# Context expert rows summed on TensorE inside two-head attention steps: a hybrid HGRN2, attention and PEER layer pair on one core

## What is computed

```python
def attend(q, k, v):                       # latent: k, v = 512 latent + 128 cached context positions
    def block(qi):
        s = jnp.einsum('bqkgd,bskd->bkgqs', qi, k).astype(jnp.float32) * ATTN_SCALE
        p = jax.nn.softmax(s, axis=-1).astype(v.dtype)
        return jnp.einsum('bkgqs,bskd->bqkgd', p, v)
...
def peer_mixer(h, w_query, sub_keys, u_tab, v_tab):
    q = (x @ w_query).reshape(T, PEER_HEADS, 2, PEER_HALF)
    ...                                    # two top-16 lists, their 256 sums, top 16: expert, gate
    def block(args):
        xb, eb, gb = args
        a = jax.nn.gelu(jnp.einsum('td,thkd->thk', xb, u_tab[eb]), approximate=False)
        return jnp.einsum('thk,thkd->td', gb * a, v_tab[eb])
```

## Time and profile before

| | |
|---|---|
| median of 3 runs | 5605.55 us (5605.12 to 5608.3) |
| span of the profiled execution | 5604.2 us, the median of the runs is 1.35 us above it |
| TensorE busy, 17704 instructions | 4557.5 us, 81% |
| VectorE busy | 3712.8 us, 66% |
| ScalarE busy | 1424.7 us, 25% |
| GpSimd busy | 2184.8 us, 39% |
| moved by DMA | 1703.74 MB, mean 304 GB/s |

### The profile page before, as it was taken

One profiled execution on the slowest core, in us unless ns is written; L12 is line 12 of the kernel. 1 busy time (PEld: TensorE's weight loads), 2 busy tenths in 40 slices (PEclk: granted clock), 3 DMA queues, 4 the chain that ended last, 5 costly groups with the idle time before them and its releaser, 6 DMA issues. The chain is left out here.

```text
span 5604.2 us, 60591 instructions
## 1 busy us (share of the span) xinstructions
PE 4557.5 (81%) x17704; PEld 2520.6 (45%) x17704; DVE 3712.8 (66%) x7028; ACT 1424.7 (25%) x3646; POOL 2184.8 (39%) x1826
## 2 busy tenths in 40 slices
PE   7889988888676777777787999888795878777776
PEld 6556655646343322222265566556463433223222
DVE  2357768867788766754532677788677877677545
ACT  2112213411011333333321112134100113333333
POOL 0002124642656454455400121246336554444554
PEclk9999998999888999999999999989897989999999
DMA  7755336785989999999967543457869889999998
GB/s 267 266 184 194 122 131 219 255 331 215 384 318 346 421 419 418 418 421 416 383 225 275 197 163 117 175 191 254 330 243 365 326 311 421 421 419 411 421 421 345
DMA packets 296082, 1703.74 MB, mean 304 GB/s; under 512 B 33360, under 2 KB 43216, under 8 KB 175696
## 3 DMA queue, kind: packets, MB, share of 16 engines
q0 software_dynamic: 258048, 1342.29, 61.3%
q1 hardware_dynamic: 23712, 338.18, 15.8%
q10 hardware_dynamic: 14000, 19.42, 1.0%
HBM read 1694.52 MB, written 5.24 MB: 303 GB/s over the span
## 5 line engine op out<-in xcount | busy, mean ns | idle before, releaser
L368 POOL DMA_INDIRECT arena<-in_peer_uv,eidx x1024 | 1184.3, 1157 | 1458.7 <-POOLq L367 1195.4
L2151 DVE SCALAR_TENSOR_TENSOR arena<-arena 128x1024 f32<-128x1024 f32 x384 | 470.6, 1225 | 349.9 <-DMA arena<-in_peer_uv,eidx 338.4
L861 PE MATMUL banks<-arena 128*128 128x512 f32 x896 | 502.1, 643 | 237.7 <-PEq L1473 234.2
L411 POOL DMA_INDIRECT arena<-in_peer_uv,eidx x384 | 490.3, 1277 | 501.0 <-POOLq L410 475.7
L863 PE MATMUL banks<-arena 128*128 128x512 f32 x896 | 477.8, 616 | 0.0
L834 PE MATMUL banks<-ring,arena 128*128 128x512 f32 x864 | 383.7, 599 | 110.0 <-PEq L816 110.0
L463 ACT ACTIVATE arena<-arena 128x1 f32<-128x1 f32 (+1 forms) x772 | 156.9, 203 | 1035.4 <-ACTq L462 1033.6
L861 PEld LDWEIGHTS banks<-arena 128*128 128x128 f32 x896 | 155.3, 198 | 549.7 <-issue 549.2
L468 ACT ACTIVATE arena<-ident,arena 128x128 f32<-128x128 f32 x832 | 333.6, 401 | 234.7 <-ACTq L467 230.2
L2151 DVE SCALAR_TENSOR_TENSOR ring<-ring,arena 128x1024 f32<-128x1024 f32 x192 | 235.4, 1226 | 211.1 <-DMA ring<-in_peer_uv,eidx 209.9
L2161 DVE SCALAR_TENSOR_TENSOR arena<-arena 128x1024 f32<-128x1024 f32 x256 | 306.9, 1225 | 95.3 <-DMA arena<-in_peer_uv,eidx 80.8
(11 more groups left out here) (303 smaller groups left out, 7763.1 us busy)
## 6 DMA issues: line engine op xcount, KB each, us to landing
ring<-in_wblk SPq DMA_DIRECT2D x160, 2048.0 KB
arena<-in_peer_uv,eidx POOLq DMA_INDIRECT x1408
arena<-in_lnrows ACTq DMA_DIRECT2D x6, 1024.0 KB, 9.5
arena<-in_sk ACTq DMA_DIRECT2D x4, 1024.0 KB, 7.4
hT<-in_peer_uv,eidx POOLq DMA_INDIRECT x192
ring<-in_peer_uv,eidx POOLq DMA_INDIRECT x192
x<-in_x_sample ACTq DMA_DIRECT2D x1, 2048.0 KB, 28.6
out<-arena ACTq DMA_DIRECT2D x4, 512.0 KB, 7.5
```

The lines of the kernel that those rows point to most:

```text
L368: nc.gpsimd.indirect_dma_start(grow[j], None, ins["peer_uv"], bass.IndirectOffsetOnAxis(ap=eidx[:, n, r:r + 1].bitcast(U32), axis=0)).then ...
L411: nc.gpsimd.indirect_dma_start(gslot[j], None, ins["peer_uv"].rearrange("(e h) d -> e (h d)", h=2), bass.IndirectOffsetOnAxis(ap=eidx[:, n ...
L861: nc.tensor.matmul(banks[:, b, :], diag[n], row[:, 0:CB], start=start, stop=stop, skip_group_check=True).then_inc(diag_used, 1)
L2151: V.scalar_tensor_tensor(u, u, 1.0, h2[:, t - 2, :], ALU.mult, ALU.mult, accum_out=av[:, r:r + 1])
```

## The change

- **Steps for units.** An attention step treats both heads of a pair for 128 queries: 32 steps instead of 64 units. Scores of the two heads are issued in turn (rows 0 to 63 and 64 to 127 of the array); the weighing has the values as the stationary side (64 columns), so the result comes out transposed, head by head in 64 partitions of bank 5. The reciprocal sums are spread by two more matmuls, copied by ScalarE (`sums_out`) and multiplied in by VectorE (`finish`) straight into `oattT`. The output transposes and GpSimd's staging of queries go; queries are transposed from `qkv`, one block in each step. The probabilities' ten transposes go through bank 4 alone in three parts (4, 4, 2 and the query block).
- **Sums of context rows on TensorE.** Ids are permuted (`ctx_ids`, `dot_column`) so that one gather brings four slots for 32 tokens. Four such gathers make a group. `ctx_group(n)` multiplies each with a 128 x 32 weight block (`spread_weights`) into its own 32 partitions of banks 6 and 7: eight matmuls of 512 columns in each step. VectorE's v-row additions and `merge_sums` go.
- **Dots** use `rep`, a replica of 32 rows of `h2c` in all four partition quarters, fetched by four DMAs from ScalarE's queue for every 16 dots. They use six slots, at the end three. Sum rows use seven slots, four of them in `ring[:, 1]`. SyncE therefore holds the next block for slot 1 until the last group is done (`ring_given`).
- **Halves.** Dots, GELU and weights are handled in two halves of 64 slots; the first half's GELU comes at the start of stage 5.
- **Row counts.** 16 rows in stage 3 instead of 24, 7 in each head instead of 6, then 22 and 4; the last 30 dots in steps 0 to 12. No row is left for `one_mix(one_tile)`.
- **Scalings.** The four constant scalings of a head's gates (`decays`) move from VectorE to ScalarE (`keys_in`).

```diff
-GATE_ROWS = 24
-HEAD_ROWS = 6
+GATE_ROWS = 16
+HEAD_ROWS = 7
 KEY_ROWS = 22
 QUERY_ROWS = 4
-UNIT_ROWS = 2
+STEP_ROWS = [3] + [2] * 6 + [3] * 2 + [2] * 3 + [3]
+DOT_SLOTS, LATE_SLOTS, SUM_SLOTS = 6, 3, [3, 4, 5, 12, 13, 14, 15]
...
                 for n, b in enumerate(CTX_BLOCKS + LAT_BLOCKS + ONE_BLOCKS + GRP_BLOCKS):
+                    if n == len(CTX_BLOCKS + LAT_BLOCKS) + 1:
+                        assert n % 2 == 1
+                        sp.wait_ge(ring_given, 1)
+                        sp.sem_inc(ring_given, -1)
                     load(n % 2, l * NB + b)
...
+            def ctx_rows_in():
+                dot_rows(0, dots_end + LATE_SLOTS)
+                pool.wait_ge(ring_idle, 1)
+                pool.sem_inc(ring_idle, -1)
+                sum_rows(0, len(SUM_SLOTS))
+                dots, sums = dots_end + LATE_SLOTS, len(SUM_SLOTS)
+                for n in range(1, STEPS):
+                    last = min(SLOTS, dots_by(n) + LATE_SLOTS)
+                    dot_rows(dots, last)
+                    dots, last = last, min(SLOTS, len(SUM_SLOTS) + REPS * n)
+                    sum_rows(sums, last)
+                    sums = last
...
+                def keys_in(b, d, h):
+                    bank, n = 5 + d, (l * 2 + d) * HEADS + h
+                    keys, keep = unit(decayed[b], LAT, keysum[d]), unit(keep1[b], LAT, d)
                     arrived(bank)
+                    nc.scalar.activation(keys, banks[:, bank, :], ACT.Sigmoid, scale=-1.0)
+                    nc.scalar.activation(keep, banks[:, bank, :], ACT.Sigmoid).then_inc(bank_free[bank], 1)
+                    act.drain()
+                    nc.scalar.activation(keys, keys, ACT.Copy, scale=omlb[:, n:n + 1])
+                    nc.scalar.activation(keep, keep, ACT.Identity, bias=lbf[:, n:n + 1], scale=omlb[:, n:n + 1])
                     act.drain().then_inc(gate_ready, 1)
...
+                for n in range(STEPS):
+                    more = n + 1 < STEPS
+                    if n == gelu_step:
+                        ctx_gelu(1)
+                    turned_block(n, 0, 4)
+                    turned_block(n, 4, 8)
+                    if more:
+                        exponentials(n + 1, 0)
+                        exponentials(n + 1, 1)
+                    if n:
+                        sums_out()
                     arrived(4)
+                    if n + LT < STEPS:
+                        m = n + LT
+                        nc.scalar.copy(qTs[m // LT % 2][:, m % LT * P:(m % LT + 1) * P], query_bank)
+                    nc.scalar.copy(PT[n % 2][:, 8:10, :], at_bank(4, 2)).then_inc(bank_free[4], 1)
+                    act.drain().then_inc(turned_ready, 1)
+                    if n in (1, 10):
+                        square_root(LT * 4)
...
+                def ctx_group(q):
+
+                    if q % BUILD == 0:
+                        pe.wait_ge(blocks_ready, 1)
+                        pe.sem_inc(blocks_ready, -1)
+                    weights = blocks[q // BUILD % 2].rearrange("p (q j t) -> p q j t", q=BUILD, j=REPS)
+                    for j in range(REPS):
+                        r = REPS * q + j
+                        pe.wait_ge(row_full[row_slot(1, r)], landed[l, 1, r])
+                    for half in range(2):
+                        for j in range(REPS):
+                            slot = row_slot(1, REPS * q + j)
+                            op = nc.tensor.matmul(banks[32 * j:32 * j + 32, 6 + half, :], weights[:, q % BUILD, j, :],
+                                                  row_buf[slot][:, half * CB:(half + 1) * CB],
+                                                  start=q == 0, stop=q == QG - 1, skip_group_check=True)
+                            if half:
+                                op.then_inc(row_free[slot], 1)
...
+                for n in range(STEPS):
+                    for half in range(2):
+                        pe.wait_ge(prob_ready[half], 1)
+                        pe.sem_inc(prob_ready[half], -1)
+                    turn(n, 0, 4)
+                    if n + 1 < STEPS:
+                        score(n + 1)
+                    turn(n, 4, 8)
+                    if n:
+                        weigh(n - 1)
+                    if n + LT in (4 * LT, 6 * LT):
+                        pe.wait_ge(qn_ready, 1)
+                        pe.sem_inc(qn_ready, -1)
+                    turn(n, 8, 10)
+                    ctx_group(n)
+                pe.drain().then_inc(ring_given, 1)
+                weigh(STEPS - 1)
...
+                lowest(0)
+                for n in range(STEPS):
+                    if n + 1 < STEPS:
+                        lowest(n + 1)
+                    invert(n)
+                    if n:
+                        finish(n - 1)
+                    if n == 0:
+                        dve.wait_ge(ctx_gated, 1)
+                        dve.sem_inc(ctx_gated, -1)
+                        weigh_rows(0)
+                    if n == gelu_step + 1:
+                        weigh_rows(1)
+                    spread_ahead(n)
+                    batch, part = (0, n) if n < 7 else (1, n - 9)
+                    if 0 <= part < 7:
+                        head_norm(512 + 256 * batch, 4, P, part, *narrow)
+                        if part == 6:
+                            dve.drain().then_inc(qn_ready, 1)
+                    if n < len(STEP_ROWS):
+                        ctx_rows(STEP_ROWS[n])
+                finish(STEPS - 1)
```

534 lines of the change are left out of this document (286 added, 248 removed).

## The result

The changed kernel takes 5644.54 us (median of 4 runs, 5642.24 to 5649.5) beside 5605.34 us of the kernel before (4 runs): a ratio of 1.0076, 95% interval 1.0059 to 1.0092. It is slower by 0.8%, where the forecast was 0.7% faster and its range ended at 5625. Its profiled execution spans 5642.9 us, 38.7 us more than that of before. Three of the four runs of before are those of its profile above; the fourth took 5600.48 us. A ratio to that one alone would be 1.0079, so the mix doesn't change the answer.

The account below looks back on a forecast made before the run. Attention was held bounded by VectorE (88% busy), TensorE nearly level; late stages by DMA. Layer 1 - 22.8 and layer 2 - 19.1 from 5604.2 give 5562.3, plus 1.35 is 5563.7, rounded 5564; own range 5540 to 5590, whole range 5510 to 5625.

Parts of the forecast that it names:

- A group on TensorE, and halves: Attention step on TensorE: four column tiles run together, 1.72 us a group; two tiles of 64 at half price.
- rivals 1 and 4: Attention on TensorE: rival 1, halves in turn, 5629 us, chance 0.17; rival 4, group not parallel, 5778 us, chance 0.05.
- A step on VectorE, and the gathers: Early attention steps: VectorE's order and GpSimd's gathers give 8.5 us for 12 steps, 9.2 for the first, 111 us.
- Rival 2: Early attention steps: sum rows stand behind dot rows waiting for VectorE, 9.9 us a step, 5598 us; chance 0.15.
- A step on ScalarE: Late attention steps: ScalarE's chain of copies and exponentials takes 7.2 us for each of 19 steps, 137 us.
- Cover: Attention's end into mixing: 3.7 us tail plus 7.1 us first block hide SP's wait for slot 1, cost 0.
- Key stage: Key and query stage: two fewer rows in stock cost + 2.5 us; query transposes start at 890.3, not 888.7.
- Only four stages can move: Whole layer: late stages are DMA-bound and unchanged; only heads, key and query stage, attention and single-tile mixing can move.
- Heads: Latent scan heads: the seventh row costs + 1.15 us a head, + 9.2 a layer; scalings on ScalarE hidden.
- mixing: Single latent tile's mixing: with no rows left, 62.3 us instead of 74.3, - 12.0 in layer 1.
- Gates: Before the heads: eight fewer rows end VectorE's gate work 9.2 us earlier; gain limited to TensorE's wait, 3.1 us.
- The clock: Attention steps: granted clock taken as 0.96, as in the steady part of the profile before.

Follow-up runs that it names:

- e3: Changed kernel with each step's sum rows issued before its dot rows on GpSimd; ratio 1.0014 to the kernel before.
- e2: Changed kernel without the gathers of the last 30 context dot rows of a layer; 5564.01 us, ratio 0.9929 to the kernel before.
- e1: Changed kernel without the 128 gathers of context sum rows in each layer, groups multiplying old data; ratio 0.9816 to the kernel before.
- e18: e15 run again, on the same chip as e16; ratio 0.9937 to the kernel before.
- e16: Repeat of e5 with ScalarE copying the last probabilities and query block before the reciprocals; 5558.33 us, ratio 0.9928 to the kernel before.
- e5: e3 with ten slots instead of seven for sum rows once the last dot is done; ratio 1.0000 to the kernel before.
- e7: e5 with 24 context rows in the gates and six in each head again; ratio 1.0013 to the kernel before.
- e15: The kernel of e16 with the context half's first GELU moved behind the key copies on ScalarE; ratio 0.9995 to the kernel before.
- e8: e3 with each context sum row gathered only half as long, 2 KB instead of 4 KB; ratio 0.998 to the kernel before.

## Why the prediction was wrong

- *A group on TensorE, and halves*: right. A group takes 1.92 us for 1.72, and the two heads' tiles overlap, so rivals 1 and 4 are out.
- *The step that failed* is "A step on VectorE, and the gathers". It took 8.5 us for an early step, from VectorE's order and GpSimd's throughput. An early step took 11.6. From the first transposes at 904.44 to the end of group 12 at 1052.3 it was 147.9 us instead of 111: + 36.9 of the 44.5. I counted GpSimd's time for each gather and forgot the time from issue to landing, 5.3 to 6.5 us, behind which the group and all of TensorE's queue stand. Of the 3.1 us that an early step was over the forecast, mending GpSimd's order takes away 1.7 (e3), leaving out the last dots' gathers 3.2 (e2), and leaving out the sum rows 4.1 (e1). VectorE's own work and order, kept in e1, need no more than 7.5 us. Rival 2 had the mechanism and priced only issue "and some wait": 9.9 us. e3 has 9.9 too, but with that order mended, so the number is a coincidence; its ratio is 1.0014, where 5598 meant 0.9987.
- *A step on ScalarE*, 7.2 us: right by number (7.6; the 19 steps took 145.1 us instead of 140) and wrong by reason. ScalarE's chain lets a step pass in 6.2 us (e1), at which TensorE is nearly full, and the wait for the fourth row made 7.6 of it. The count of slots against the group's size was in the code and in no term of the sum, so the nearness of 7.2 is luck.
- *Cover*: SP's wait for slot 1, priced at 0, is 0: the second block starts with 0.41 us idle. Tail 5.6 instead of 3.7 us.
- *Key stage*: + 4.9 for + 1.6. The last of its first 22 context rows starts 5.05 us later (+ 2.5 forecast; the heads' 2.1 us later end is in it), VectorE waits 1.32 us for a replica of `h2c` that I had costed at 0, and 1.79 us where ScalarE loads a table for the root:

```profile
862.96 1.28 ACT L509 ACT_TABLE_LOAD   x1 [17.30 <-ACTq L508]
...
864.62 0.25 DVE L2183 RECIPROCAL small<-small 128x16 f32<-128x16 f32 x1 [1.79 <-DVEq L2182]
...
875.27 1.23 DVE L1987 SCALAR_TENSOR_TENSOR arena<-arena 128x1024 f32<-128x1024 f32 x1 [1.32 <-DVEq L1985]
```

  Moving the GELU didn't gain it: e18 isn't faster than e16.
- *Only four stages can move*: wrong by - 16.8 us. The last stages of layer 2 became shorter, here and in e2, e3 and e5 to e18. Without this the miss would have been larger.
- *Heads* + 8.1 (+ 9.2 forecast) and *mixing* - 10.8 (- 12.0): right. *Gates* - 6.0 instead of - 3.1: the idle time in front of one matmul was not all that the rows had cost; e7 gives 7.4 us for eight rows, near to VectorE's 9.2.
- *The clock* was taken as 0.96 from the steady part before. It fell to 0.70 in a stretch where e1, without the sum rows' gathers and waits, has 0.91, and this made each wait dearer: a group after a long wait costs 3.6 us.

The Trainium skill, page TensorEngine Tiling (Array Packing), section Tiling Modes, says that a change of mode drains TensorE. The trace of e1 shows steps of 6.2 us with all their changes where 6.05 was summed with 0.10 us for each, so the milder price held. (The prediction's estimate by that rule, 6.6 and 8.9 us, comes to 6.4 and 8.8 by its own terms.) Its page DMA: Bandwidth & Descriptors, section Latency and other measured facts, gives about 2 us as the fixed cost of a DMA. The moving of the bytes comes on top of that. A gather is 128 rows of 4 KB, 0.52 MB; at the 278 GB/s of the late steps that is 1.9 us, so an estimate by the page is 3.9 us. The shortest landing of a gather in the changed kernel's late steps took 4.1 us, near to it; the medians, with other gathers in flight, are 5.3 to 6.5 us, and here the measured value decides.

## What to carry over

An operation that needs several gathered rows at once waits for the last of them: price it by the landing time under load (here 4.1 us at the least, 5.3 to 6.5 in the medians), look at what the issuing queue does ahead of that last row, and count its slots against the group: with seven slots for groups of four the last row waited for the present group, with ten it didn't. (Eight were not run.) Put the transfers that an in-order engine waits for first in the issuing queue, and the ones with a stock behind them last. And before two kernels are compared over different chips or sessions, compare the same kernel over them.

## What the runs showed that was not expected

- Two kinds of chips, or of sessions: each chip was used in one. On three of six, TensorE's pauses in a late group end 0.92 to 1.07 us after GpSimd's last gather of a row, and a finished matmul reaches ScalarE mostly 1.2 to 1.3 us after it; on the other three no late group has such a pause. The traces of the first three hold 42,800 to 44,600 semaphore updates where those of the others hold 49,500 (kernels with all gathers). One kernel (e15, e18) differs by 0.6% between them. What ties the engines together there isn't settled. It isn't a wait in the program, and it goes away neither with half the bytes of the sum rows (e8) nor with ScalarE's other order (e15).
- Four column tiles of 32 by 512 run together at full rate: 16 f32 passes in 1.92 us, measured over hundreds of groups. Two tiles of 64 run together too (1.31 us for 20 passes of 128, 2.1 in turn).
- TensorE's granted clock is 1.00 over 80 us without gathers (e1) and 0.85 in the same stretch with them: it falls with the waits, and makes a stall dearer than its length.
- A gather of 128 rows of 4 KB takes 5.3 to 5.6 us to land in the median at 905 to 980 us (DMA share 0.68 for 889 to 980), 6.0 to 6.5 at 980 to 1060 (0.83), both with six gathers in a step, and 5.7 in the late steps with four (0.82).
